# Given tables, a software pipeline and a second copying engine in the S5 input stage of a hybrid encoder

## The chip, the core and the metric

One Trainium2 chip, one of its cores, one program. The metric is the device time of one execution in microseconds (us), the median of several. TensorE (PE) multiplies and transposes, VectorE (DVE), ScalarE (ACT) and GpSimd (POOL) do elementwise work, SyncE (SP) issues most transfers. SBUF is the on-chip memory of 128 partitions; PSUM, eight banks of 128 x 512 fp32, takes what TensorE writes.

## The reference

Two layers over 1040 rows of 1024 numbers. The first has attention beside a state-space layer (S5) whose inputs `u` are turned into complex states by a matrix per group and direction, and then scanned. Of it, this matters here:

```python
a_bar = jnp.exp(a * dt)
b_bar = ((a_bar - 1.0) / a)[..., None] * lax.complex(b_re[direction].astype(f32), b_im[direction].astype(f32))
bu = jnp.einsum('blgp,gnp->blgn', ug.astype(jnp.complex64), b_bar)
_, states = lax.associative_scan(_linear_combine, (a_seq, bu), axis=1, reverse=reverse)
```

There are 64 groups of 16 inputs, 64 states a group, two directions.

## The kernel before

The kernel is a row of stages, each a block with one instruction list per engine and a barrier at its end. Three matter here.

`front` projects the rows: 36 units of 128 output columns, TensorE without a pause. A unit's three pieces sit in PSUM until they are taken out; unit u + 2 writes the same place. Eight units give `u`, four the keys and values, and then come eight heads of three units: `q` (VectorE normalises it, the rows of L1709 to L1718), gate `a` and gate `b` (ScalarE's sigmoid, then VectorE multiplies, L1726). Behind the gates VectorE builds half tables with `complex_table` (six operations of 128 x 512 each, L770 to L775): 16 that a later stage needs (`tab_d`), and `2 * EARLY` for `s5_states` (`tab_in_d`), spread over the gates by `made_after`, two buffers, stored by SP.

`s5_states` makes the inputs of the scan, eight steps of the sequence at a time. The 64 groups go in eight blocks of eight. For a block, a table of powers of `a_bar` times `B` (real and imaginary, 128 x 2 x 8 x 8 x 16) is needed in `table[:, n % 2]`: the first two come from `tab_in_d`, VectorE builds six in a loop of two, 128 x 1024 per operation. TensorE transposes it (L846) in four lots m = 0 to 3 of four transposes into two alternating banks `tp`; ScalarE copies a bank to the weights `wl` ("w_in" in the rows, L874). When all four are copied, TensorE multiplies for each of the eight groups (L855, L857: two column halves for two directions; four matmuls, each of them two records) into one of four banks `zp`, and ScalarE copies that to `Z` (L879). Each engine takes the block's steps in that order, transposes first, then sums, with signals `turned`, `copied`, `summed`, `stored` between them and `built` for tables. `us` holds all of `u`.

`heads` then runs the attention, with the scan of `Z` on GpSimd beside it. `Steps` signals each VectorE operation; called as `do(...)` it makes the next instruction wait for this one, as `do.free(...)` it does not.

Of the kernel before, what the change touches and what calls it, by code (L numbers as in the profile page):

```python
# [21 lines left out]
P = 128  # L22
KC = D // P
HEADS, KV, HD = 8, 2, 128
G, GP, NS = 64, 16, 64
T = P // GP
CH = L // T
# [320 lines left out]
EARLY = 2  # L348
# [429 lines left out]
def s5_states(nc, c, d, t, gates_stored):  # L778

    with stage(nc) as s:  # L780
        us = s.sb("us", [P, G, CH])
        table = s.sb("tab", [P, 2, 2, GB, T, GP])
        tmp = s.sb("tmp", [P, 2, GB, T, GP])
        wl = s.sb("w_in", [P, GB, 2, P])
        tp = [s.ps(f"tp{b}", 512) for b in range(2)]
# [3 lines left out]
        built = s.flag("table_built")  # L789
        turned = s.flag("turned", per=4, credit=8)  # L790
        copied = s.flag("weights_copied", per=4, credit=4)
        summed = s.flag("summed", per=GB, credit=GB)
        stored = s.flag("stored", per=GB, credit=GB)
        steps = s.sem("dve_steps")
        uv = d["u"].rearrange("s p g c -> (s p) g c")
        with nc.Block() as block:  # L796
            @block.sync
            def _(sp):
                for n in range(G // GB):
                    if n < EARLY:  # L800
                        if n:
                            for half in range(2):
# [3 lines left out]
                        for half in range(2):  # L806
                            g = slice(half * GB // 2, (half + 1) * GB // 2)
                            sp.dma_start(table[:, n % 2, :, g].rearrange("p q g s f -> p q (g s f)"),
                                         d["tab_in"][n][:, :, half, :]).then_inc(tab_loaded[half], 16)
                    if n >= 2:  # L810
                        sp.wait_ge(loaded[n % 2], 16 * (n // 2))
                    g = slice(n * GB, (n + 1) * GB)
                    sp.dma_start(us[:, g, :], uv[:, g, :]).then_inc(loaded[n % 2], 16)

            @block.vector
            def _(dve):
                do = Steps(dve, steps)
                do.free(nc.vector.memset(t["Z"][:, 0, :, :], 0.0))
                with do.loop((G // GB - EARLY) // 2, 12) as i:
                    for b in range(2):  # L820
                        n = i * 2 + b + EARLY

                        turned.wait(dve, n, -4)
                        g = bass.ds(n * GB, GB)
                        do(complex_table(nc.vector, do, table[:, b], tmp,
                                         t["pw_in"][:, :, :, g].rearrange("p s q g -> p q s g"),
                                         t["B"][:, :, g, :], 1))
                        dve.sem_inc(built.sem, 1)

            @block.tensor  # L830
            def _(pe):
                turned.start(pe)
                summed.start(pe)
                f, r = slice(0, NS), slice(NS, P)
                for nb in range(G // GB):
                    b = nb % 2
                    if nb >= EARLY:
                        built.wait(pe, nb - EARLY, 1)
                    for m in range(4):
                        if nb < EARLY and m % 2 == 0:  # L840
                            pe.wait_ge(tab_loaded[m // 2], 16 * (nb + 1))

                        copied.wait(pe, nb, m - 1)
                        for n in range(4):
                            g, q = 2 * m + n // 2, n % 2
                            last = nc.tensor.transpose(tp[m % 2][:, n * P:(n + 1) * P],  # L846
                                                       table[:, b, q, g].rearrange("p s q -> p (s q)"), c["ident"][:, :])
                        last.then_inc(turned.sem, 1)
                    copied.wait(pe, nb, 4)
                    pe.wait_ge(loaded[b], 16 * (nb // 2 + 1))  # L850
                    for g in range(GB):
                        stored.wait(pe, nb, g - 3)
                        for q in range(2):
                            cols = slice(q * CH, (q + 1) * CH)
                            nc.tensor.matmul(zp[g % 4][f, cols], wl[:, g, q, f], us[:, nb * GB + g, :],  # L855
                                             start=True, stop=True)
                            last = nc.tensor.matmul(zp[g % 4][r, cols], wl[:, g, q, r], us[:, nb * GB + g, ::-1],  # L857
                                                    start=True, stop=True)
                        last.then_inc(summed.sem, 1)

            @block.scalar
            def _(act):
                copied.start(act)
                stored.start(act)
                for b in range(2):
                    act.wait_ge(gates_stored[b], 16 * HEADS)
                with act.Fori(0, G // GB // 2) as i:
                    for b in range(2):
                        nb = i * 2 + b
                        for m in range(4):  # L870
                            turned.wait(act, nb, m + 1)

                            summed.wait(act, nb, 2 * m + 2 - GB)
                            nc.scalar.activation(wl[:, 2 * m:2 * m + 2, :, :].rearrange("p g q m -> p (g q m)"),  # L874
# [2414 lines left out]
```

## Time and profile before

| | us |
|---|---|
| median of 3 runs (2682.29 to 2682.92) | 2682.81 |
| profiled execution, its own time | 2685.11 |
| its span | 2683.3 |
| PE busy | 2501.9 (93%) |
| DVE busy | 1432.0 (53%) |
| ACT busy | 976.6 (36%) |
| POOL busy | 1145.5 (43%) |

Times in a row count from the start of the span. Busy shares average over all stages; what a change in one stage is worth is read in that stage, from who waits for whom. In a timeline row "x8" is eight instructions merged, the second number the time from the first's start to the last's end, and the bracket the engine's idle time ahead and the work whose end released it.

### The profile page before, as it was taken

Reading aid. Unit: us, or ns where it says so; the run is one execution under the profiler, and the core shown is the slowest. Engines: PE = TensorE matmul, PEld = TensorE weight load, DVE = VectorE, ACT = ScalarE, POOL = GpSimd, SP = SyncE. Lnnn points to the kernel's source line nnn. Section 1 sums busy time; section 2 is a strip of 40 time slices with the busy share of each in tenths; the row PEclk is TensorE's granted clock in tenths of the full one; section 3 lists DMA queues with packets and bytes.
Section 4 is the critical chain, followed back from the end, with each engine's and each line's share of the span. In section 5 each row is a group of like instructions: output and inputs, shape, how many; then the busy total and the mean of one; then the engine's idle time right before and its main releaser. Section 6 shows DMA issues by size and latency. Waiting matters only on the chain. (4 is left out here: it accounts for less than half of the span.)

```text
span 2683.3 us, 40555 instructions
## 1 busy us (share of the span) xinstructions
PE 2501.9 (93%) x15206; PEld 2164.7 (81%) x15206; DVE 1432.0 (53%) x2120; ACT 976.6 (36%) x2130; POOL 1145.5 (43%) x1114
## 2 busy tenths in 40 slices
PE   6999999779998879999999999999898899999998
PEld 6988888678887669777788887887776699999787
DVE  6459887657776545415654543556555452222414
ACT  5232222756664121323332333265565420000331
POOL 3545452067776246322135444343343255554330
PEclk9999999889999989999999999999998899999999
DMA  7424443311112674535333433534334264443544
GB/s 167 106 80 132 145 147 103 117 42 36 49 41 98 160 190 138 192 118 175 98 117 123 151 124 134 177 116 151 136 107 170 73 241 156 143 140 132 171 157 157
DMA packets 272216, 349.27 MB, mean 130 GB/s; under 512 B 45700, under 2 KB 212254, under 8 KB 269990
## 3 DMA queue, kind: packets, MB, share of 16 engines
q1 hardware_dynamic: 236422, 268.85, 32.3%
q10 hardware_dynamic: 35616, 78.00, 8.0%
q8 instruction: 118, 1.93, 0.3%
q14 instruction: 60, 0.49, 0.1%
HBM read 223.23 MB, written 114.03 MB: 126 GB/s over the span
## 5 line engine op out<-in xcount | busy, mean ns | idle before, releaser
L1164 POOL TENSOR_TENSOR w_hi<-w_raw,ones 128x512 fp32r<-128x512 f32 (+1 forms) x232 | 289.0, 1246 | 736.9 <-PE r L1175 324.8
L1175 PE MATMUL r<-h_lo,w_hi 128*128 128x264 f32 (+1 forms) x1200 | 395.6, 330 | 5.1 <-PEq L224 5.1
L1175 PE MATMUL r<-h_hi,w_lo 128*128 128x264 f32 (+1 forms) x1200 | 387.2, 323 | 0.0
L1175 PE MATMUL r<-h_hi,w_hi 128*128 128x264 f32 (+1 forms) x1200 | 386.5, 322 | 0.0
L1166 POOL TENSOR_TENSOR w_lo<-w_raw,w_hi 128x512 fp32r<-128x512 f32 (+1 forms) x232 | 355.2, 1531 | 18.2
L1175 PEld LDWEIGHTS r<-h_lo,w_hi 128*128 128x128 f32 x1200 | 227.2, 189 | 26.6 <-issue 7.6
L1175 PEld LDWEIGHTS r<-h_hi,w_hi 128*128 128x128 f32 x1200 | 227.2, 189 | 21.3 <-issue 2.4
L1175 PEld LDWEIGHTS r<-h_hi,w_lo 128*128 128x128 f32 x1200 | 227.2, 189 | 17.6
L499 POOL TENSOR_TENSOR w_lo<-room,w_hi 128x512 fp32r<-128x512 f32 x64 | 87.1, 1388 | 193.3 <-ACT w_hi L586 193.3
L1905 PE MATMUL o<-v,prob 116*116 116x129 f32 (+1 forms) x1296 | 166.1, 274 | 0.3 <-ACT prob L1955 0.3
L1905 PEld LDWEIGHTS o<-v,prob 116*116 116x116 f32 (+1 forms) x1296 | 158.3, 180 | 3.9 <-ACT prob L1955 0.5
L895 POOL TENSOR_TENSOR scan<-Z,room 128x256 f32<-128x256 f32 x130 | 96.4, 742 | 144.6 <-POOLq L796 100.5
L1175 PE MATMUL sums<-h_lo,w_hi 128*128 128x264 f32 (+1 forms) x432 | 155.5, 360 | 1.7 <-PEq L409 1.7
L1175 PE MATMUL z<-h_lo,w_hi 128*128 128x264 f32 (+1 forms) x384 | 146.7, 382 | 4.9 <-PEq L2220 3.6
L3218 DVE TENSOR_TENSOR buffer<-buffer 128x1040 f32<-128x1040 f32 x16 | 25.4, 1588 | 216.9 <-ACT buffer L3195 216.9
L1175 PE MATMUL sums<-h_hi,w_lo 128*128 128x264 f32 (+1 forms) x432 | 139.7, 323 | 0.0
L1175 PE MATMUL sums<-h_hi,w_hi 128*128 128x264 f32 (+1 forms) x432 | 139.3, 323 | 0.0
L1175 PE MATMUL z<-h_hi,w_hi 128*128 128x264 f32 (+1 forms) x384 | 127.5, 332 | 0.0
L1175 PE MATMUL z<-h_hi,w_lo 128*128 128x264 f32 (+1 forms) x384 | 127.4, 332 | 0.0
L1175 PE MATMUL r<-xc_hi,w_lo 128*128 128x264 f32 (+1 forms) x384 | 123.6, 322 | 0.0
L1175 PE MATMUL r<-xc_hi,w_hi 128*128 128x264 f32 (+1 forms) x384 | 123.1, 321 | 0.0
L1175 PE MATMUL r<-xc_lo,w_hi 128*128 128x264 f32 (+1 forms) x384 | 123.0, 320 | 0.0
(398 smaller groups left out, 6213.9 us busy)
## 6 DMA issues: line engine op xcount, KB each, us to landing
w_raw<-in_w_in_even SPq DMA_DIRECT2D x72, 256.0 KB, 3.4
w_raw<-in_w_in_odd SPq DMA_DIRECT2D x64, 256.0 KB, 3.6
w_raw<-in_w_ogate SPq DMA_DIRECT2D x64, 256.0 KB, 2.7
v_d<-vs ACTq DMA_DIRECT2D x8, 1152.0 KB, 4.2
us<-u_d SPq DMA_DIRECT2D x16, 520.0 KB, 5.4
xc_d<-xc ACTq DMA_DIRECT2D x8, 1040.0 KB, 6.3
qk_d<-qk ACTq DMA_DIRECT2D x16, 520.0 KB, 2.7
qk<-qk_d SPq DMA_DIRECT2D x8, 1040.0 KB, 5.0
```

Source lines behind the costliest of these rows:

```text
L499: nc.gpsimd.tensor_tensor(w[1][:, at % HK, cols], wr[:, at % 2, cols], w[0][:, at % HK, cols].bitcast(F32), ALU.subtract).then_inc(wl_done, 1)
L895: do(tt(tmp[:, :, :, :], now.broadcast_to([P, 2, 2, G]), t["step"][:, :, :].rearrange("p (o q) g -> p o q g", o=2), ALU.mult))
L1164: self.nc.gpsimd.tensor_tensor(hi, raw, one, ALU.mult).then_inc(self.hi_done, 1)
L1166: self.nc.gpsimd.tensor_tensor(lo, raw, hi.bitcast(F32), ALU.subtract).then_inc(self.split, 1)
L1175: ins = self.nc.tensor.matmul(bank[:, 0:n], w[:, u % self.buffers, k, :], z[:, off:off + n], start=(first and k == 0 and w is self.hi and ...
L1905: last = nc.tensor.matmul(o_slot(w)[0:m, :], sb[0:kn, n % NB, k, i * m:(i + 1) * m], vt[0:kn, k, g, :], start=(k == 0), stop=(k == NT - 1))
L3218: do(v.tensor_tensor(og[:, b, :], og[:, b, :], cz[:, b, :], ALU.mult))
```

## The change

`EARLY` goes from 2 to 3: `front` builds six half tables for `s5_states` instead of four, and VectorE builds five tables in the stage instead of six. `table` gets four buffers, `wl` two, `tp` four banks, one for each m; `us` is halved. TensorE's lots of transposes for block nb + 1 are put behind groups 1, 3, 5 and 7 of block nb. VectorE takes the weight copies of m = 3 and, in odd blocks, of m = 2 (`act_copies` says which are ScalarE's), and its table operations are single steps between these copies, five a block. No loops are left.

```diff
-EARLY = 2
+EARLY = 3
...
-        us = s.sb("us", [P, G, CH])
-        table = s.sb("tab", [P, 2, 2, GB, T, GP])
+    NB, HB, TB = G // GB, GB // 2, 4
+
+    def act_copies(nb, m):
+        return m < 2 or (m == 2 and nb % 2 == 0)
+        us = s.sb("us", [P, G // 2, CH])
+        table = s.sb("tab", [P, TB, 2, GB, T, GP])
-        wl = s.sb("w_in", [P, GB, 2, P])
-        tp = [s.ps(f"tp{b}", 512) for b in range(2)]
+        wl = s.sb("w_in", [P, 2, GB, 2, P])
+        tp = [s.ps(f"tp{m}", 512) for m in range(4)]
...
+        def copy_weights(eng, copy, nb, m):
+            eng.wait_ge(turned, 4 * nb + m + 1)
+            if nb >= 2:
+                eng.wait_ge(summed, GB * (nb - 2) + 2 * m + 2)
+            copy(wl[:, nb % 2, 2 * m:2 * m + 2, :, :].rearrange("p g q m -> p (g q m)"),
+                 tp[m][:, :]).then_inc(copied[m], 1)
...
+                        for half in range(2):
+                            if n:
                                 sp.wait_ge(tab_loaded[half], 16 * n)
-                        if n >= 2:
-                            sp.wait_ge(turned.sem, turned.per * (n - 1) + turned.credit)
...
+                    if n >= NB // 2:
+                        sp.wait_ge(summed, GB * (n - NB // 2 + 1))
...
+                def table_step(n, i):
+                    g = slice(n * GB, (n + 1) * GB)
+                    q, second = divmod(i, 3)
+                    if i == 0 and n >= TB:
+                        dve.wait_ge(turned, 4 * (n - TB + 1))
+                    if second == 2:
+                        do(tt(table[:, n % TB, q], tmp[:, 0], tmp[:, 1], ALU.add if q else ALU.subtract))
+                        if q:
+                            dve.sem_inc(built, 1)
+                        return
+                    power = t["pw_in"][:, :, second, g].rearrange("p s g -> p g s").unsqueeze(3)
+                    x = t["B"][:, second ^ q, g, :].unsqueeze(2)
+                    do(tt(tmp[:, second], power.broadcast_to([P, GB, T, GP]), x.broadcast_to([P, GB, T, GP]), ALU.mult))
+
                 do.free(nc.vector.memset(t["Z"][:, 0, :, :], 0.0))
-                with do.loop((G // GB - EARLY) // 2, 12) as i:
-                    for b in range(2):
-                        n = i * 2 + b + EARLY
-
-                        turned.wait(dve, n, -4)
-                        g = bass.ds(n * GB, GB)
-                        do(complex_table(nc.vector, do, table[:, b], tmp,
...
+                for b in range(2):
+                    dve.wait_ge(gates_stored[b], 16 * HEADS)
+
+                def some_steps(first, count):
+                    for at in range(first, min(first + count, 6 * (NB - EARLY))):
+                        table_step(EARLY + at // 6, at % 6)
+
+                for nb in range(NB):
+                    for m in range(4):
+                        if nb:
+                            some_steps(5 * nb + m, 1)
+                        if not act_copies(nb, m):
+                            copy_weights(dve, nc.vector.tensor_copy, nb, m)
+                    if nb:
+                        some_steps(5 * nb + 4, 1)
+                    else:
+                        some_steps(0, 5)
...
+                def turn(nb, m):
+                    if nb < EARLY:
+                        pe.wait_ge(tab_loaded[m // 2], 16 * (nb + 1))
+                    else:
+                        pe.wait_ge(built, nb - EARLY + 1)
+                    if nb:
+                        pe.wait_ge(copied[m], nb)
...
+                for m in range(4):
+                    turn(0, m)
+                for nb in range(NB):
+                    pe.wait_ge(loaded[nb % 2], 16 * (nb // 2 + 1))
                     for g in range(GB):
-                        stored.wait(pe, nb, g - 3)
+                        n = GB * nb + g
+                        pe.wait_ge(copied[g // 2], nb + 1)
+                        if n >= 4:
+                            pe.wait_ge(stored, n - 3)
...
+                        last.then_inc(summed, 1)
+                        if g % 2 and nb + 1 < NB:
+                            turn(nb + 1, g // 2)
...
+                for m in range(4):
+                    if act_copies(0, m):
+                        copy_weights(act, copy, 0, m)
+                for n in range(G):
+                    nb, g = divmod(n, GB)
+                    act.wait_ge(summed, n + 1)
+                    nc.scalar.activation(t["Z"][:, 1:CH + 1, :, n:n + 1].rearrange("p c q g -> p q (c g)"),
+                                         zp[n % 4][:, 0:2 * CH].rearrange("p (q c) -> p q c", q=2),
+                                         ACT.Copy).then_inc(stored, 1)
+                    if g % 2 and nb + 1 < NB and act_copies(nb + 1, g // 2):
+                        copy_weights(act, copy, nb + 1, g // 2)
```

What VectorE has to do in `s5_states` before: one table, in the loop (L770 to L775 are the steps of `complex_table`; ISA and REGISTER_ALU rows are waits and addresses).

```order
L770 ISA [waits turned_129]
L770 REGISTER_ALU
L770 TENSOR_TENSOR tmp<-room 128x1024
L771 ISA
L771 TENSOR_TENSOR tmp<-room 128x1024
L84 ISA
L772 TENSOR_TENSOR tab<-tmp 128x1024 [waits dve_steps_133]
L84 REGISTER_ALU
L773 TENSOR_TENSOR tmp<-room 128x1024 [waits dve_steps_133]
L774 TENSOR_TENSOR tmp<-room 128x1024
L84 REGISTER_ALU
L775 TENSOR_TENSOR tab<-tmp 128x1024 [waits dve_steps_133]
```

And in the changed kernel, in block 1 and the first steps of block 2 (there L841 is a product, L835 a sum or difference, L804 the weight copy; `tp_120` is the bank of m = 2, `tp_121` that of m = 3).

```order
L841 TENSOR_TENSOR tmp<-room 128x1024 [waits dve_steps_138,turned_131]
L841 TENSOR_TENSOR tmp<-room 128x1024 [waits dve_steps_138]
L804 COPY w_in<-tp_120 128x512 [waits turned_131,dve_steps_138]
L835 TENSOR_TENSOR tab<-tmp 128x1024
L804 COPY w_in<-tp_121 128x512 [waits turned_131,dve_steps_138]
L841 TENSOR_TENSOR tmp<-room 128x1024
L841 TENSOR_TENSOR tmp<-room 128x1024 [waits dve_steps_138]
L835 TENSOR_TENSOR tab<-tmp 128x1024 [waits dve_steps_138]
```

Two weight copies have come between the steps; every step waits for the one before it, at the latest through the copy's wait, and no step waits for a copy.

TensorE between two blocks before, from the last group of block 0 (L857) to the first of block 1 (L855), without the repeats of the first lots:

```order
L857 MATMUL zp_123<-us,w_in 64x130
L846 MATMUL tp_118<-ident,tab 128x128 [waits weights_copied_130,table_half0_loaded_126]
L846 MATMUL tp_118<-ident,tab 128x128 x3
L846 MATMUL tp_119<-ident,tab 128x128 [waits weights_copied_130]
L846 MATMUL tp_119<-ident,tab 128x128 x3
L846 MATMUL tp_118<-ident,tab 128x128 [waits weights_copied_130,table_half1_loaded_127]
L846 MATMUL tp_118<-ident,tab 128x128 x3
L846 MATMUL tp_119<-ident,tab 128x128 [waits weights_copied_130]
L846 MATMUL tp_119<-ident,tab 128x128 x3
L855 MATMUL zp_120<-us,w_in 64x130 [waits stored_132,u_loaded1_125,weights_copied_130]
```

The changed kernel, TensorE in block 1 from the end of group 1 to the start of group 4 (L875 is the transpose for block 2, L890 and L892 the matmuls):

```order
L892 MATMUL zp_123<-us,w_in 64x130
L875 MATMUL tp_118<-ident,tab 128x128 [waits weights_copied0_132,table_half0_loaded_128]
L875 MATMUL tp_118<-ident,tab 128x128 x3
L890 MATMUL zp_124<-us,w_in 64x130 [waits stored_137,weights_copied1_133]
...
L892 MATMUL zp_125<-us,w_in 64x130
L875 MATMUL tp_119<-ident,tab 128x128 [waits weights_copied1_133,table_half0_loaded_128]
L875 MATMUL tp_119<-ident,tab 128x128 x3
L890 MATMUL zp_122<-us,w_in 64x130 [waits stored_137,weights_copied2_134]
```

The sixteen transposes that stood together, each lot behind a copy, now stand four at a time behind two groups, and a group waits for its own copy alone.

## Rows read from the trace of the kernel before

**Rows 1.** The page's first line.

```profile
span 2683.3 us, 40555 instructions
```

**Rows 2.** Stretches: length, busy (x) of PE, PEld, DVE, ACT, POOL, clock, DMA.

```profile
272.00:308.00 36.00, 36.00 (x224) 32.13 (x223) 29.92 (x27) 9.68 (x17) 17.88 (x12) 1.00 0.47 140
481.00:487.00 6.00, 5.73 (x60) 5.73 (x62) 5.90 (x6) 3.72 (x7) 0.00 (x0) 0.57 0.81 302
508.00:515.00 7.00, 5.86 (x82) 5.14 (x80) 6.13 (x6) 5.80 (x13) 0.00 (x0) 1.00 0.01 2
```

**Rows 3.** Timeline, ScalarE and GpSimd: start us, us, engine, line, work.

```profile
503.85 1.08 ACT L874 ACTIVATE w_in<-tp 128x512 f32<-128x512 f32 x2 [0.34 <-PE tp L846]
534.14 3.76 ACT L879 ACTIVATE Z<-zp 128x260 f32 x8 [0.85 <-PE zp L857]
...
538.77 0.72 POOL L895 TENSOR_TENSOR scan<-Z,room 128x256 f32<-128x256 f32 x1 [100.49 <-POOLq L796]
```

**Rows 4.** Timeline of TensorE in `s5_states`.

```profile
476.58 0.69 PE L846 MATMUL tp<-ident,tab 128*128 128x128 f32 x2 [8.38 <-DMA tab<-tab_in_d]
...
501.56 1.09 PE L846 MATMUL tp<-ident,tab 128*128 128x128 f32 x8
503.08 1.14 PE L846 MATMUL tp<-ident,tab 128*128 128x128 f32 x8 [0.43 <-ACT w_in L874]
504.99 0.33 PE L855 MATMUL zp<-us,w_in 128*64 128x130 f32 x1 [0.77 <-ACT w_in L874]
...
508.49 0.27 PE L857 MATMUL zp<-us,w_in 128*64 128x130 f32 x1
508.69 0.33 PE L846 MATMUL tp<-ident,tab 128*128 128x128 f32 x1
...
533.34 0.33 PE L855 MATMUL zp<-us,w_in 128*64 128x130 f32 x1 [0.77 <-ACT w_in L874]
...
536.84 0.27 PE L857 MATMUL zp<-us,w_in 128*64 128x130 f32 x1
```

**Rows 5.** Timeline of VectorE in `s5_states`, its first table.

```profile
480.78 1.23 DVE L770 TENSOR_TENSOR tmp<-room 128x1024 f32 x1 [9.11 <-PE tp L846]
481.92 1.22 DVE L771 TENSOR_TENSOR tmp<-room 128x1024 f32 x1
483.18 1.23 DVE L772 TENSOR_TENSOR tab<-tmp 128x1024 f32<-128x1024 f32 x1
...
486.83 1.23 DVE L775 TENSOR_TENSOR tab<-tmp 128x1024 f32<-128x1024 f32 x1
```

**Rows 6.** Timeline of VectorE, two copies from PSUM in the second layer.

```profile
1404.19 0.68 DVE L2460 COPY kt<-sums 128x512 f32<-128x512 f32 x1
1404.79 0.68 DVE L2460 COPY kt<-v 128x512 f32<-128x512 f32 x1
```

**Rows 7.** Timeline of VectorE in `front`, heads 0 to 2.

```profile
195.16 1.96 DVE L1709 TENSOR_TENSOR work<-work,scratch 128x1040 f32<-128x1040 f32 x1
...
215.81 0.69 DVE L770 TENSOR_TENSOR staged<-room,C 128x512 f32<-128x512 f32 x1 [0.15 <-DVE staged L775]
...
223.67 1.84 DVE L1726 TENSOR_TENSOR work<-work,r 128x264 f32<-128x264 f32 x3 [0.15 <-DVE table L775]
...
232.58 2.04 DVE L1709 TENSOR_TENSOR work<-work,scratch 128x1040 f32<-128x1040 f32 x1 [0.22 <-DVE staged L775]
...
267.69 1.77 DVE L1709 TENSOR_TENSOR work<-work,scratch 128x1040 f32<-128x1040 f32 x1 [0.22 <-DVE table L775]
```

**Rows 8.** Timeline of SyncE's issues, tables in `s5_states`.

```profile
471.41 1.26 SPq L808 DMA_DIRECT2D tab<-tab_in_d  x2
...
478.44 1.17 SPq L808 DMA_DIRECT2D tab<-tab_in_d  x2
```

**Rows 9.** Timeline of ScalarE in `front`, last pieces of `q`, heads 1 and 2.

```profile
227.53 0.48 ACT L1467 ACTIVATE work<-r,cols_a 128x264 f32<-128x264 f32 x1 [1.74 <-PE r L1175]
...
263.55 0.48 ACT L1467 ACTIVATE work<-r,cols_a 128x264 f32<-128x264 f32 x1 [1.74 <-PE r L1175]
```

More of the change, by code:

```diff
@@ L788, in s5_states @@
         tab_loaded = [s.sem(f"table_half{half}_loaded") for half in range(2)]
[L789 to L793, printed above, removed]
+        built = s.sem("table_built")
+        turned = s.sem("turned")
+        copied = [s.sem(f"weights_copied{m}") for m in range(4)]
+        summed, stored = s.sem("summed"), s.sem("stored")
         steps = s.sem("dve_steps")
         uv = d["u"].rearrange("s p g c -> (s p) g c")
+        def copy_weights(eng, copy, nb, m):
[4 more added lines that the diff above has]
+                 tp[m][:, :]).then_inc(copied[m], 1)
         with nc.Block() as block:
@@ L817, in _ @@
                 do = Steps(dve, steps)
[L818 to L828 removed]
+                tt = nc.vector.tensor_tensor
@@ L830, in _ @@
             @block.tensor
             def _(pe):
-                turned.start(pe)
-                summed.start(pe)
                 f, r = slice(0, NS), slice(NS, P)
[L835 to L850, printed above, removed]
+                def turn(nb, m):
[5 more added lines that the diff above has]
+                        pe.wait_ge(copied[m], nb)
+                    for n in range(4):
+                        g, q = 2 * m + n // 2, n % 2
+                        last = nc.tensor.transpose(tp[m][:, n * P:(n + 1) * P],
+                                                   table[:, nb % TB, q, g].rearrange("p s q -> p (s q)"), c["ident"][:, :])
+                    last.then_inc(turned, 1)
@@ L858, in _, with copy @@
                                                     start=True, stop=True)
-                        last.then_inc(summed.sem, 1)
+                        last.then_inc(summed, 1)
+                        if g % 2 and nb + 1 < NB:
+                            turn(nb + 1, g // 2)
             @block.scalar
             def _(act):
-                copied.start(act)
-                stored.start(act)
+                def copy(out, given):
+                    return nc.scalar.activation(out, given, ACT.Copy)
@@ L865, in _ @@
                 for b in range(2):
                     act.wait_ge(gates_stored[b], 16 * HEADS)
[L867 to L874, printed above, removed]
-                                                 tp[m % 2][:, :], ACT.Copy).then_inc(copied.sem, 1)
-                        for g in range(GB):
-                            summed.wait(act, nb, g + 1)
-                            gg = bass.ds(nb * GB + g, 1)
-                            nc.scalar.activation(
-                                t["Z"][:, 1:CH + 1, :, gg].rearrange("p c q g -> p q (c g)"),
-                                zp[g % 4][:, 0:2 * CH].rearrange("p (q c) -> p q c", q=2),
-                                ACT.Copy).then_inc(stored.sem, 1)
+                for m in range(4):
+                    if act_copies(0, m):
+                        copy_weights(act, copy, 0, m)
```

16 lines of the change are left out of this document (6 added, 10 removed).

## The prediction

> **What bounds the kernel now.** The profiled execution has a span of 2683.3 us [rows 1]; its own time was 2685.11 us, 1.8 above the span, and 2.3 above the median of the three timed runs, 2682.81. The change is worth what it takes out of, or adds to, that span.
>
> I read the busy time by stretches first, to see who is the bound where the edits fall. In the projection stage ahead (`front`) TensorE is busy 36.00 of 36.00 us at full clock while VectorE has 29.92; in `s5_states` nobody is full: 5.86 of 7.00 us for TensorE, 6.13 for VectorE, 5.80 for ScalarE at a clock of 1.00 [rows 2]. So `front` is TensorE's and the reader should ask there only whether VectorE's extra work can make TensorE wait. `s5_states` is a chain of waits, and its end is what counts: the first scan on GpSimd starts at 538.77, 0.87 after ScalarE's last copy of Z ends, and everything behind starts from that barrier [rows 3]. A microsecond off the stage is a microsecond off the kernel.
>
> Then TensorE's own timeline, where the loop repeats. Block 4's transposes start at 508.69, block 3's at 501.56: 7.13 us a block [rows 4]. Inside: eight transposes in 1.09 (the last lasts 0.27, so one per 0.117), 0.43 idle for a copy of the weights, eight more, 0.77 idle for the last copy, then 3.70 of matmuls (504.99 to 508.69). Without the idle stretches TensorE needs 3.70 + 16 x 0.117 = 5.57. The eight blocks end at 536.84 + 0.27 = 537.11, the last one's matmuls having begun at 533.34, so 3.77 [rows 4]; ScalarE's last copy ends 0.79 later, at 537.90 [rows 3].
>
> VectorE in the same stage has no copies. It waits until the first block is turned and builds from 480.78 [rows 5]. TensorE's waits inside a block are all put down to ScalarE's copies [rows 4], so VectorE, busy 6.13 of 7.00, is near the bound and not the bound.
>
> **What the change does to each engine.** TensorE does the same 128 transposes and 256 matmuls. What goes is its idle time for the copies: four transposes of the next block stand behind every second group, into a bank of their own, and the weights have two buffers. That removes 0.43 + 0.77 = 1.20 a block. It adds switches between transposes and matmuls, eight a block for two. A switch costs about 0.09: from the last matmul at 508.49 to the transpose at 508.69 is 0.20, where the 32 matmul pairs of a block follow in 3.70 / 32 = 0.116 [rows 4]. Bounds: nothing, and 0.2; I take 0.09, so 6 x 0.09 = 0.5, and 6.1 us for a block nobody holds up.
>
> VectorE loses one table of six but takes twelve of the 32 weight copies (bank 3 of every block, bank 2 of every odd one; of these 9 lie before its last table step). A table step now always waits for the step before: start to start 1.26 (481.92 to 483.18), against 1.14 where the old code let the second product follow the first freely (480.78 to 481.92) [rows 5]. 30 steps x 1.26 = 37.8. The trace has no VectorE copy from `tp`, but it has the same shape from another PSUM tile: 0.68 each, the next starting after 0.60 [rows 6]. A step behind a copy does not wait for it (the order rows show no wait there), so 0.60 stands for a copy; the bounds are 0.60 and 0.72 (0.69 plus a waited gap of 0.03). Signalling a finished table costs 0.12 more: the gap in front of a step behind a signal is 0.15 where others have 0.03 [rows 7].
>
> *Does VectorE keep up?* From block 1 to block 5 it does 5 steps and 1 or 2 copies: 5 x 1.26 + 0.60 = 6.9 or 7.5, mean 7.2 with the signals 7.3. TensorE needs 6.1. So VectorE becomes the bound there, at the old pace of 7.13, and the removed waits come back as TensorE waiting for copies 2 and 3 of each block. The gain can come only from the end, when VectorE has no steps left.
>
> *The sum.* VectorE's first instruction is the copy of bank 3 of block 0, which waits for the same four turned banks as its first product now, 480.78. Nothing ahead of that event changes but a half table asked for earlier. Step 0 starts at 481.38. Copy (5, 3) has 29 steps, 7 further copies and 4 signals in front of it: 481.38 + 36.54 + 4.20 + 0.48 = 522.60. It ends at 523.29 and TensorE goes on 0.06 later, at 523.35 (as at 504.99 behind ScalarE's copies, which ended at 503.85 + 1.08 = 504.93 [rows 3, 4]). Then two groups (0.93), four transposes (0.47), two switches (0.18): 524.93. Block 6 is free, 6.1: 531.03. Block 7 has no transposes behind it, 3.77: 534.80. Now it is 537.11. **Gain 2.3 us**, 2682.81 - 2.3 = 2680.5.
>
> ScalarE in the free blocks has 8 copies of Z and 2 or 3 of weights. Its eight Z copies take 3.76, the last lasting about 0.67, so at most 0.44 each; weight copies in a pair (1.08 for two) follow after 0.48 [rows 3]. 8 x 0.44 + 3 x 0.48 = 5.0, under 6.1: no bound.
>
> *Loads.* Table 0 is asked for from 471.41, and TensorE's wait for its first half ends at 476.58; table 1 is asked for at 478.44, when the second half is there [rows 4, 8]. So a half table lands 5 to 7 us after its issue. The change asks for table 1's first half at 476.6, for table 2 at about 482 to 484, and has it by about 491. TensorE would turn it from about 489.5, but stands at copy (1, 2) until VectorE ends it: 481.38 + 8 x 1.26 + 0.12 + 0.69 = 492.3. A load some microseconds late costs nothing, since VectorE's copies wait only for transposes due some 5 us before them. The halved `us` makes loads 4 to 7 wait for sums four blocks earlier; each has over 20 us.
>
> *The front.* Two more half tables are built, two more stores. One took 7.9 (215.81 to 223.67) [rows 7]; half of a table of this stage would be 3.6 (below), so 4 to 8 each. A head with three builds and its normalisation took VectorE 35.1 (232.58 to 267.69), and TensorE takes 36.02 for one (227.53 to 263.55) [rows 7, 9]. The change gives heads 2 and 5, which had two, a third; so every head but the last takes VectorE some 35.1, and it still gains 0.9 a head on TensorE. What TensorE needs is the first piece of the second gate: in head 0 it came at 223.67 for a need at 227.53. In head 1, two builds now stand in front of that piece instead of one: 232.58 + (223.67 - 195.16) = 261.1 for a need at 263.5. Slack 2.4, so the price is nothing.
>
> *A rule weighed.* [rows 5] show 1.14 for a product that waits for nothing and 1.26 for one that waits. The Trainium skill (VectorE: DVE Perf Modes, The DRAIN you can't avoid) says that instructions drain all the same and a semaphore between them costs nothing. By that rule a step would cost the mean of now, (488.06 - 480.78) / 6 = 1.21; 30 of them 36.4, and the result 2679.1. I keep the rows' 1.26, since all 30 now wait.
>
> **Rivals.**
>
> *TensorE free all through (0.06).* If steps cost less than I think, TensorE runs at its own pace: block 0, half of it at the low clock (between 5.6 and twice that), 8.5 from 480.6; six blocks of 6.1; then 3.77: 529.5. Gain 7.6, 2675.2. It needs 30 steps and 8 copies in some 38 us, 1.1 a step; no step in [rows 5] is under 1.14.
>
> *The stage breaks even or loses (0.10).* VectorE's chain has no slack at all, so every cost I have too low counts 8 to 30 times. Copy and step share no buffer, but a copy at 0.90 start to start instead of 0.60, for whatever reason, gives 8 x 0.3 = 2.4 and no gain; at 1.1, the time is 2684.5. For it: no row has a PSUM copy followed by a product. Against: the pair in [rows 6], PSUM then PSUM, at 0.60.
>
> *The front is exposed (0.04).* Once VectorE is more than the 2.4 of slack later in a head than I put it, TensorE waits for the gate's eviction and every further microsecond counts. With both added builds exposed at 4: 2680.5 + 8 = 2688.5, slower. Against: heads with three builds catch up, 35.1 to 36.0.
>
> *The clock falls (0.02).* TensorE's clock was 0.57 in 481 to 487, after 8.38 us idle up to 476.58, and 1.00 in 508 to 515 with 17% idle [rows 2, 4]; 1.00 is the 2.4 GHz level, 0.57 mostly the 1.2 GHz one. With idle stretches of 0.5 to 1.4 a block it should stay. If it sat at 1.2 GHz, a block would be nearly twice 5.6, about 11, for five blocks: 20 us more, 2700. The Trainium skill (TensorE: Matmul & The Clock Gate, Part 4: PE-mode transpose) says that transposes do not count as busy for the gate, which speaks for it, as they now stand between all matmuls. By that rule, the trace should already show less than 1.00 with a third of the work in transposes, and it doesn't.
>
> **How the numbers follow.** My forecast, VectorE the bound in blocks 1 to 5 and the end gained: 0.78, with 2678.9 to 2682.3: down by 1.5 if a step costs today's mean of 1.21 (1.21 x 30 against 37.8), up by 1.0 if a copy costs 0.72, and either way by switches (7 to 9 of them in the free part, each 0.1 off). With break-even taken in on one side and half-way to the first rival on the other, 2677.8 to 2683.2 holds 8 in 10. What a measurement of this kernel can tell is 0.2%, 5.4 us: a gain over that is only the first rival, a loss over that the front or the clock. Faster 0.07, same 0.88, slower 0.05.
>
> **What would show it.** VectorE without a gap over 0.2 from 480.8 to about 524; its copies at 0.68 to 0.69 and 0.60 to the next start; TensorE idle about 0.8 to 1.4 a block until then, released by VectorE's copies and not ScalarE's, and no more in blocks 6 and 7, 6.1 from one to the next; the last matmul near 534.8; `front` at the same 36.0 a head. It would be wrong if steps behind copies start late, if ScalarE's copies hold TensorE, or if the stage begins at another time than 471.4.

## The result: 0.16% slower, and the profile after

The median of 20 runs is 2687.6 us (2683.06 to 2690.45); the kernel before, on the same chip and in the same rounds, has 2682.57 (20 runs). The ratio of after to before is 1.0016, with a 95% interval of 1.0010 to 1.0022: 4.3 us lost (2.7 to 5.9), where a gain of 2.3 was forecast. The profiled executions hide it: 2684.87 us after, 2685.11 before, one from the faster end of its runs and one from the slower. So the total of two traces says nothing here; their stages do.

The page after, span and first lines of the busy times:

```profile
span 2683.0 us, 40407 instructions
PE 2498.3 (93%) x15206; PEld 2155.9 (80%) x15206; DVE 1459.9 (54%) x2138; ACT 972.8 (36%) x2118; POOL 1137.9 (42%) x1114
```

Three stretches to set beside those of [rows 2] (a head of the front, the stage's first block with the clock coming back, its middle; each row is the length, then the busy time of PE, PEld, DVE, ACT and POOL, the clock, and the DMA share and rate):

```profile
276.00:312.00 36.00, 36.00 (x224) 32.13 (x223) 33.64 (x32) 9.55 (x18) 17.97 (x12) 1.00 0.43 141
485.00:491.00 6.00, 5.02 (x62) 3.93 (x58) 5.86 (x6) 4.23 (x8) 0.00 (x0) 0.96 0.76 259
508.00:515.00 7.00, 5.96 (x74) 4.63 (x74) 6.68 (x7) 5.57 (x11) 0.00 (x0) 1.00 0.17 65
```

VectorE has 33.6 of 36.0 us in a head where it had 29.9 (this head has a third build now), and 6.68 of 7.00 in the stage where it had 6.13.

**Two landmarks** cut the program. The front is taken from TensorE's first turn of `c` (116.65 us before, 118.62 after; that start differed by 1.0 and 1.4 us between the two traces of each of these kernels, and lies at 116.5 to 119.0 in all) to VectorE's memset of Z. The stage of the states is taken from that memset to GpSimd's first scan (538.77 in [rows 3]). After:

```profile
475.87 0.17 DVE L843 MEMSET Z<- 128x128 f32 x1 [3.10 <-PEq L1320]
541.02 0.72 POOL L928 TENSOR_TENSOR scan<-Z,room 128x256 f32<-128x256 f32 x1 [99.45 <-POOLq L807]
```

and before, the memset that the 538.77 stands against:

```profile
471.51 0.17 DVE L818 MEMSET Z<- 128x128 f32 x1 [2.42 <-PEq L1287]
```

So the front went from 471.51 - 116.65 = 354.9 to 475.87 - 118.62 = 357.2 us, **2.4 longer**, and the stage from 67.3 to 65.1, **2.1 shorter**.

**The stage runs as forecast.** VectorE in it, and the end of its work there:

```profile
484.89 0.69 DVE L804 COPY w_in<-tp 128x512 f32<-128x512 f32 x1 [8.85 <-PE tp L875]
485.50 2.48 DVE L841 TENSOR_TENSOR tmp<-room 128x1024 f32<-128x1024 f32 x2
488.01 1.23 DVE L835 TENSOR_TENSOR tab<-tmp 128x1024 f32<-128x1024 f32 x1
...
495.68 0.69 DVE L804 COPY w_in<-tp 128x512 f32<-128x512 f32 x1
496.29 1.22 DVE L835 TENSOR_TENSOR tab<-tmp 128x1024 f32<-128x1024 f32 x1
...
526.79 0.69 DVE L804 COPY w_in<-tp 128x512 f32<-128x512 f32 x1
```

A copy lasts 0.69 and the next instruction starts 0.61 after it starts; two steps take 2.51 (485.50 to 488.01). Copy (5, 3) starts 41.90 behind the first copy; the forecast's sum has 522.60 - 480.78 = 41.82. Besides the loads of the two first tables (9.2 and 1.0 us), what TensorE waits for is VectorE, 3.5 us in all:

```profile
PE tp L875 <- DMA tab<-tab_in_d: 10.2, 2, 9.2
PE zp L890 <- DVE w_in L804: 3.5, 8, 0.9
```

and its end (the first row goes on behind copy (5, 3); the last one is the last matmul):

```profile
527.53 0.33 PE L890 MATMUL zp<-us,w_in 128*64 128x130 f32 x1 [0.16 <-DVE w_in L804]
...
528.57 0.66 PE L875 MATMUL tp<-ident,tab 128*128 128x128 f32 x4
529.16 0.33 PE L890 MATMUL zp<-us,w_in 128*64 128x130 f32 x1
...
530.20 0.66 PE L875 MATMUL tp<-ident,tab 128*128 128x128 f32 x4
...
539.15 0.27 PE L892 MATMUL zp<-us,w_in 128*64 128x130 f32 x1
```

A pair of groups with its four transposes takes 1.63 (528.57 to 530.20) where nobody holds it, so a free block takes 6.5 and not 6.1.

**The front does not.** VectorE, heads 1 and 2 of 0 to 7 (start, us; the idle time in brackets). The row of line 1742 opens a head's normalisation, as those of line 1709 do in [rows 7]; 263.13 is the first piece of head 1's second gate:

```profile
234.55 2.04 DVE L1742 TENSOR_TENSOR work<-work,scratch 128x1040 f32<-128x1040 f32 x1 [0.22 <-DVE staged L775]
...
263.13 1.84 DVE L1759 TENSOR_TENSOR work<-work,r 128x264 f32<-128x264 f32 x3
...
273.04 1.24 DVE L1742 TENSOR_TENSOR work<-work,scratch 128x1040 f32<-128x1040 f32 x1 [0.22 <-DVE table L775]
...
288.69 0.69 DVE L770 TENSOR_TENSOR staged<-room,C 128x512 f32<-128x512 f32 x1
...
292.08 1.77 DVE L774 TENSOR_TENSOR staged<-room,C 128x512 f32<-128x512 f32 x1
...
300.53 1.26 DVE L1759 TENSOR_TENSOR work<-work,r 128x264 f32<-128x264 f32 x2
...
310.02 1.24 DVE L1742 TENSOR_TENSOR work<-work,scratch 128x1040 f32<-128x1040 f32 x1 [0.22 <-DVE staged L775]
```

Head 1 takes VectorE 38.49 us (234.55 to 273.04) and head 2 takes 36.98, where TensorE needs 36.02: it is idle for 0.52 at most in a row in head 2, and falls behind. An operation of 128x512 values lasts 0.69 alone (288.69) and up to 1.77 while GpSimd splits weights beside it (292.08):

```profile
291.69 1.61 POOL L1199 TENSOR_TENSOR w_lo<-w_raw,w_hi 128x512 fp32r<-128x512 f32 x1
```

The Trainium skill (GPSIMD Engine Reference, 2. Architecture) says that GpSimd's read port to SBUF is shared with VectorE; the 0.69 and 1.77 agree. Over the 132 such operations of the 22 builds in this trace, all 77 that overlap no work of GpSimd last 0.68 to 0.69 us, and the 55 that do have a mean of 1.45, a few of them at 0.69 too. No run took the splits away, so the cause of the 1.77 is read from this overlap.

Who is held by a late gate piece of VectorE is ScalarE, ahead of its roots (waits in the front, then its timeline):

```profile
ACT L1525 <- DVEq L1760: 5.9, 5, 1.4
```

```profile
301.54 0.48 ACT L1500 ACTIVATE work<-r,cols_a 128x264 f32<-128x264 f32 x1 [1.74 <-PE r L1208]
...
303.26 1.28 ACT L1525 ACT_TABLE_LOAD   x1 [0.95 <-DVEq L1760]
...
337.56 0.48 ACT L1500 ACTIVATE work<-r,cols_a 128x264 f32<-128x264 f32 x1 [1.74 <-PE r L1208]
...
373.96 0.48 ACT L1500 ACTIVATE work<-r,cols_a 128x264 f32<-128x264 f32 x1 [1.74 <-PE r L1208]
...
410.31 0.48 ACT L1500 ACTIVATE work<-r,cols_a 128x264 f32<-128x264 f32 x1 [1.74 <-PE r L1208]
```

The rows of line 1500 follow TensorE's last piece of `q` in a head, as [rows 9] do. They are of heads 3 to 6. Up to 337.56 they are 36.02 apart, then 36.40 and 36.35, and 36.69 to head 7: behind head 4, VectorE's lateness has reached TensorE. These are 1.4 of the 2.4 us; the rest comes behind that. In the heads of the trace before, no wait of ScalarE is for VectorE's gate.

### The profile page after: what moved, and what is told of

It is laid out like the page before. It is cut to its first block and busy times, and to the rows that moved or that the text cites. A ratio compares the mean times of both kernels' runs of the same rounds, so it can differ in the third digit from the quotient of the medians.

```text
span 2683.0 us, 40407 instructions
## 1 busy us (share of the span) xinstructions
PE 2498.3 (93%) x15206; PEld 2155.9 (80%) x15206; DVE 1459.9 (54%) x2138; ACT 972.8 (36%) x2118; POOL 1137.9 (42%) x1114
```

## The experiments

"Front" and "stage" are the lengths between the landmarks in each run's own trace; the ratio is to the kernel before in the same rounds. Lines with + and - are against the changed kernel unless another base is named.

| kernel | front | stage | median, us (runs) | ratio, 95% interval |
|---|---|---|---|---|
| before, unchanged (`base_again`) | 354.9 | 67.1 | 2683.63 (11) | 0.9999, 0.9989 to 1.0008 |
| `after_again` | 357.2 | 65.1 | 2688.88 (11) | 1.0018, 1.0009 to 1.0027 |
| `front_only` | 357.3 | 64.9 | 2687.11 (11) | 1.0007, 0.9998 to 1.0016 |
| `early_start` | 354.9 | 62.7 | 2682.08 (11) | 0.9995, 0.9986 to 1.0004 |
| `front_four` | 359.4 | 64.0 | 2687.97 (9) | 1.0022, 1.0012 to 1.0032 |
| `one_then_two` | 354.9 | 65.4 | 2682.80 (11) | 1.0004, 0.9995 to 1.0013 |
| `three_ahead` | 357.2 | 62.4 | 2683.41 (11) | 1.0005, 0.9996 to 1.0014 |
| `late_stage` | 355.7 | 67.3 | 2685.22 (11) | 1.0012, 1.0003 to 1.0021 |
| `warm_before` | 354.9 | 64.8 | 2680.67 (11) | 0.9998, 0.9989 to 1.0007 |
| `warm_after` | 357.3 | 65.5 | 2687.27 (9) | 1.0021, 1.0011 to 1.0031 |
| `both_mended` | 354.9 | 62.4 | 2684.06 (11) | 0.9999, 0.9990 to 1.0008 |
| `both_warm` | 354.9 | 62.4 | 2683.45 (11) | 1.0002, 0.9993 to 1.0011 |
| `warm_before_2` | 354.9 | 67.4 | 2682.53 (12) | 0.9995, 0.9985 to 1.0005 |
| `warm_one` | 354.9 | 63.9 | 2683.84 (12) | 1.0004, 0.9995 to 1.0012 |
| `stage_alone` | 354.9 | 77.1 | 2693.80 (6) | 1.0038, 1.0023 to 1.0052 |
| `fewer_steps` | 354.8 | 59.7 | 2677.29 (12) | 0.9978, 0.9970 to 0.9987 |

**Both kernels again**, to see what repeats.

> The kernel before once more, unchanged, with a trace of its own. It tells how far one traced execution of the same program differs from another, stage by stage. Theory A (the front pays for the tables): the last sigmoid of the projection stage near 468, the first scan near 539, as in the first trace, within 0.5 us; what differs by more is no property of the change. Rival B (the traces of before and after differ by chance in the front too): the front end moves by 2 to 4 us here as well.

> The changed kernel once more, with a second trace. A: again about 4 us slower than before in the median; TensorE's heads 3 to 7 of the front again over 36.0 us each, 1.7 us in sum, and the stage with the tables again 1.8 us shorter. B: the front's lateness is elsewhere or absent in this trace.

The loss repeats (1.0018), and so do front and stage to 0.2 us. What does not repeat is behind the stage: from the first scan to the end the two traces of before differ by 3 us (2144.5 and 2141.6), and the two of after as well (2142.0 and 2145.1). That stretch is 2141.4 to 2145.4 in the seven traces with the old stage code and 2140.1 to 2149.2 in the eleven with the new. So a total of one trace can't show a difference of a few us, and the medians of the runs have to.

**The front alone.** The kernel before, with a third given table built and stored, not used:

```
+GIVEN = 3
-    jobs = [("out", n) for n in range(2 * G // GB)] + [("in", n) for n in range(2 * EARLY)]
+    jobs = [("out", n) for n in range(2 * G // GB)] + [("in", n) for n in range(2 * GIVEN)]
```

> Only the front builds and stores the third table's two halves (GIVEN = 3), spread over the gates as in the change; the stage behind is that of before and reads two tables, so the third is stored and not used. A: the front pays, so this is slower than before by the change's loss plus the 1.8 us that the stage gained, 4 to 6 us (2687 to 2689). Rival C (the stage or what it leaves behind pays, not the front): within 1 us of before. The prediction on record said 0 for this part.

The 2.4 us of the front are all there. The run shows less than was expected: by its ratio 1.9 us (-0.5 to 4.3) over the kernel before, where 4 to 6 had been expected, and by itself that excludes neither theory. The stage, whose code is the old one, took 64.9 instead of 67.1 to 67.3, which nobody expected; it is taken up below. Front and stage together take 422.2 us here and 422.1 in the kernel before: in this trace the stage gave back what the front lost.

**A fourth table in the front** (`GIVEN = 4` on the same base).

> The stage stays as before and loads two tables; the front builds and stores four of them (24 half tables instead of 20), two of which nobody reads. Theory A (VectorE's work is what bounds heads 1 to 6 of the front once it has three builds in each): heads 0 and 5 get a fourth build of some 5.5 to 6 us that has no slack left to lie in, so the front from the first turn of c to the Z memset takes some 357.3 + 6 to 11 = 363 to 368 us against 354.9 of the kernel before and 357.3 with three tables, and the run some 2692 to 2697 us. Rival B (a cost of 2.4 us that comes once, from one late gate or one late load of ScalarE's table): the front takes 357 to 358 us and the run stays near 2687.

The front grew by 2.1 more, not by 6 to 11. So VectorE's total is not simply the bound (theory A as stated falls), and neither does the cost come once only (rival B falls).

**The same 22 half tables, one behind gate a and two behind gate b**, where the change has two and one:

```
-        made_after[gates[n * (len(gates) - 1) // NX]].append(n)
+        made_after[gates[n // 3 * 2 + (n % 3 > 0)]].append(n)
```

> The changed kernel, with the 22 half tables put one after a head's gate a and two after its gate b in heads 0 to 6 (the last after the last gate a, as it was). The work is the same, only its place among the heads' steps is another. Theory A (the sum of VectorE's work in a head, 36 to 38.5 us, against TensorE's 36.02): the front still takes 356.5 to 358 us, and the run 2686 to 2689. Rival C (what costs is two builds in a row between gate a and the next step that ScalarE waits for): the front falls back to 354.9 to 355.5 us, and the run to some 2684 to 2686.

The front is at 354.9 again and the run at 1.0004: rival C holds, and decides the front. VectorE's busy time from 200 to 454 us, some seven heads, first in this kernel, then in the changed one:

```profile
sum 254.00, DVE 227.07; mean DVE 32.44
```

```profile
sum 254.00, DVE 239.31; mean DVE 34.19
```

That is 12.2 us more. From the first step of head 0 to that of head 7, where the list of operations is the same, it is 240.9 against 223.5 us. Of these 17.4 us, 11.5 are in the builds: as many of their operations lie beside work of GpSimd (52 here, 55 in the changed kernel), but with a mean of 1.27 us and not 1.45. So the edit shows that the place alone costs the 2.4 us; that it does so through GpSimd's splits is read from the overlaps. Three pairs differ by this edit, with other things the same: `after_again` (1.0018) and this one (1.0004), `three_ahead` and `both_mended` (1.0005, 0.9999), `warm_after` and `warm_one` (1.0021, 1.0004). The mean is 0.0012, 3.3 us, against 2.4 in the traces.

**VectorE started earlier.** `early_start` has two given tables; VectorE does 7 steps before its first copy and ScalarE takes bank 2 of every block. `three_ahead` has three tables and 6 steps ahead; `both_mended` is that with the other placement in the front.

```
-EARLY = 3
+EARLY = 2
-        return m < 2 or (m == 2 and nb % 2 == 0)
+        return m < 3
+                some_steps(0, 7)
...
-                            some_steps(5 * nb + m, 1)
+                            some_steps(2 + 5 * nb + m, 1)
```

> The stage of the change with two given tables as before, so the front is that of before. VectorE begins its first seven steps at once, without waiting for the copy of bank 3 of block 0, and takes only the copies of m = 3; ScalarE takes three banks of every block. A: the front costs nothing here and VectorE has 9 us of lead, so TensorE runs at its own 6.5 us a block; the stage ends about 5 us earlier than before and the kernel takes 2677 to 2679. C: if the pipelined stage costs something behind it, it stays within 2 us of before.

> The changed kernel, with three given tables, but VectorE does the six steps of its first table ahead of its first copy, where it stood idle for 9 us, and stays four steps further ahead from there. If the stage's rest is still VectorE's steps between TensorE's blocks, the time from the Z memset to the first scan falls from 65.1 us to 62.5 to 64, and the run to some 2683 to 2686; the front stays at 357.3 us. If the stage is bound by TensorE and ScalarE now, it stays at 65 us and the run does not change. Beside two given tables with an early start (62.8 us in the stage, 354.8 in the front) it tells what the third table costs by itself: about 2.4 us by theory A.

> The changed kernel with both mends: the half tables one behind gate a and two behind gate b, and VectorE's first six table steps ahead of its first copy. If the two are independent the front takes 354.9 us, the stage 62.4 to 62.7, and the run ends 4.7 us before that of the kernel before by its traces (67.2 in the stage), 2.5 where its clock is back early: ratio 0.998 to 0.999, some 2678 to 2680.5 us. If the later parts take back what the stage gives, as the sums of traces and medians did not agree so far by 1 to 3 us, it is at 2681 to 2683.

VectorE's 9 idle us at the stage's head are worth 2.7 us in the stage between `after_again` and `three_ahead`, and 3.0 between `one_then_two` and `both_mended`. With two given tables the early start makes 62.7 us of the 77.1 that `stage_alone` takes (below). But `early_start` missed its time: its run is 1.3 us below the kernel before (-3.8 to 1.1), where 4 to 6 had been expected; "within 2 us of before" is what its rival had said. The two mends add up in the trace (354.9 and 62.4), but not in the run: 0.9999, where 0.998 to 0.999 was expected. In that trace everything behind the first scan took 2149.2 us, 5 to 8 more than in the two of before, and no run tells why.

**A pure delay.** The kernel before, with two more multiplications behind its last gate:

```
+                for n in range(2):
+                    do(v.tensor_tensor(rs, rs, rs, ALU.mult))
```

> The kernel before, with two multiplications of 128x1040 values on VectorE added behind its last gate, so that the stage of the states starts some 2.7 us later and nothing else is changed. If a delay only adds up, the median is 2.5 to 3 us above that of the kernel before in the same rounds (ratio 1.0010). If a shift ahead of the stage makes what follows longer too (TensorE's clock falling at other places), it is 4 to 7 us above it (ratio 1.0015 to 1.0026), which would be the part of the changed kernel's loss that front and stage do not explain.

They take 2.52 us, but 1.8 of it hid in VectorE's wait for the stage's start (2.42 us before, 0.60 now), so the front grew by 0.8 only. The interval (0.8 to 5.6 us) holds that, and it holds more: inconclusive on whether a shift costs more than itself.

**TensorE kept busy before its first table**, the result not used. In `warm_before` on the kernel before, in `warm_after`, `both_warm`, `warm_one` on the changed kernel, on `both_mended` and on `one_then_two`:

```
+                for n in range(20):
+                    nc.tensor.transpose(zp[3][:, 0:P], c["ident"][:, :], c["ident"][:, :])
```

The reason is in the clock column (the third value from a row's end). In the kernel before, block 0 is summed at the 1.2 GHz level up to some 486 us:

```profile
480.00:483.00 3.00, 2.23 (x19) 1.83 (x19) 2.22 (x2) 1.41 (x3) 0.00 (x0) 0.50 0.84 268
483.00:487.00 4.00, 4.00 (x48) 4.00 (x46) 3.90 (x5) 3.06 (x6) 0.00 (x0) 0.60 0.81 315
```

and in `front_only`, with the same stage code, it is back at 2.4 GHz before the first product at 485.47:

```profile
484.00:487.00 3.00, 2.23 (x32) 1.83 (x32) 2.01 (x2) 1.88 (x4) 0.00 (x0) 0.87 0.95 316
487.00:491.00 4.00, 3.48 (x52) 3.10 (x47) 3.93 (x4) 4.00 (x9) 0.00 (x0) 1.00 0.89 301
```

In all seven traces with the old stage code the two go together: the clock back 14 to 15 us behind the memset and a stage of 67.1 to 67.4 us in four (`before`, `base_again`, `late_stage`, `warm_before_2`), back 7 to 9 us behind it and 64.0 to 64.9 in three (`front_only`, `front_four`, `warm_before`). VectorE's first table ends at 488.06 and its second begins at 490.21 in the kernel before, 2.2 us later; in `front_only` it is 492.27 and 492.75, 0.5.

> The kernel before, with 20 transposes of the identity added at the head of TensorE's program of the stage, where it otherwise stands idle for 5 us until the first table has landed; their result is not used. In the traces of the kernel before TensorE's clock is at its half level from 1 to 15 us behind the Z memset, and VectorE's second table starts 2.2 us later behind its first than it does where the clock is back 2 to 3 us sooner. Theory (half of what the changed kernel's stage seemed to gain is that state of the clock and not the change): with the clock back before block 0 the stage as it was takes 64 to 65 us from the Z memset to the first scan instead of 67.1 to 67.3, and the run 2680 to 2681 instead of 2682 to 2683. Rival (VectorE's pace alone sets the stage): it stays at 67 and the run does not change.

> The changed kernel with the same 20 idle transposes added. Its stage took 65.1 us with TensorE's clock back at full at the first product and 65.4 with it back 2 us after it, so by the theory it does not depend on the clock in block 0: it stays at 64.8 to 65.2 us, the front at 357.2, and the run at 2687 to 2688.5. Rival (TensorE's first block is on the path in it too): the stage falls by 1 us or more.

> The kernel with both mends and the 20 idle transposes. Its stage has VectorE ahead, so TensorE's first block at the half clock is on the path: with the clock back earlier the stage falls from 62.5 to 60.5 to 61.8 us and the run by some 1 to 1.5 us. If VectorE's steps or ScalarE's copies are the bound in it all the same, it stays at 62.4.

> The kernel before with 20 idle transposes ahead of its first table, once more, as the base for the next one: the stage takes 64.8 us again from the Z memset to the first scan, the front 354.9, and the run is 1.4 to 2.5 us below the kernel before.

> The changed kernel with one half table behind gate a and two behind gate b, and the 20 idle transposes: front 354.9 us, and TensorE's clock the same in block 0 as in the run before this one. Theory (at the same clock the pipeline neither gains nor loses): the stage takes 65.0 to 65.4 us, 0.2 to 0.6 more than the 64.8 of the old stage, and the run is within 1 us of the run before this one or a little above it. Rival (the pipeline gains 2 us by itself): 62.5 to 63.5 us, and 2 us below it.

In `warm_before` the old stage took 64.8 us, as expected; its run, at 0.9998, did not show the 2 us. In `warm_before_2`, the same kernel, the clock was late all the same and the stage took 67.4: the transposes don't fix the clock, but the pair shows that one code takes 64.8 or 67.4 with it. The changed stage took 65.5 in `warm_after`, with the clock back when it was without the transposes, and 63.9 in `warm_one`, which missed its expectation by 1.1. There the clock was back 4 us behind the memset and low once more from 11 to 14, so its block 0 had not the clock of `warm_before_2`, which the comparison had asked for. Where the stages are compared with a clock back early, the old one has 64.0 to 64.9 and the new one, without VectorE's steps ahead, 63.9 to 65.5: the pipeline gains nothing that is clear. In no trace with the new stage code was the clock as late as 14 us, so what the new stage takes then isn't known. `both_warm` stayed at 62.4 with the clock at full from block 0's first product, as its second expectation had it: with VectorE ahead, TensorE's first block is not the limit either. The runs say the same: `warm_one` is 1.3 us above `warm_before_2` by the medians, with intervals that overlap, and `one_then_two` (no front loss, new stage) stands at 1.0004 (0.9995 to 1.0013).

**What bounds the new stage.** `stage_alone` has `EARLY = 2`; `fewer_steps` is `one_then_two` without the four multiplications of tables 4 and 6, so those tables hold wrong values:

```
+                    if n % 2 == 0:
+                        return
```

> The changed stage with two given tables as before, so VectorE builds six tables, 36 steps, between its copies; the front as before at 354.9 us. If VectorE's steps are the bound, six more steps of 1.24 us add 6 to 7.5 us to the 65.1: 71 to 73 us, longer than the old stage's 67.2, and the run is at some 2687 to 2690. If the stage is bound by something else, it stays under 67.

> As the changed kernel with one half table behind gate a and two behind gate b, but VectorE leaves out the four multiplications of tables 4 and 6 (8 of its 30 steps; those two tables hold wrong values). If VectorE is the bound of the stage up to some 3 us, beyond which TensorE and ScalarE are, the stage falls from 65.4 us to 61.5 to 62.5, as with VectorE ahead. If it is VectorE's alone, it falls by 8 x 1.24 = 9.9 us to 55.5.

With two given tables, the new stage takes 77.1 us, 12.0 more for six steps of 1.25, where 6 to 7.5 more had been expected; the run is 10.2 us above the kernel before. TensorE now waits for whole tables:

```profile
PE tp L875 <- DVEq L837: 10.2, 5, 3.0
```

With 8 steps less it takes 59.7, 5.7 less than `one_then_two`, between the two values expected: VectorE is the bound for that much, and in this trace TensorE no longer waits for it. (Its clock was also back 3 us sooner than in `one_then_two`, so the 5.7 may not be VectorE's alone.) The run follows (5.5 us below `one_then_two`'s median, in other rounds). So this pipeline as it stands needs the third given table. The table is not the only way to give VectorE that lead: `early_start` has two and takes 62.7, with its first seven steps in the 9 us in which VectorE was idle and bank 2's copies left to ScalarE.

## Why the prediction was wrong, by its steps

**"Slack 2.4 in head 1, so the price is nothing"** is the step that failed: the cost of a head with three builds was taken as 35.1 us wherever they stand. The time of the one piece that the prediction looked at was right: 261.1 was forecast for head 1, and with the later start of the front (1.97 us) the 263.13 of the trace is that to 0.1. What came behind it was not. Head 1 took VectorE 38.49 us and head 2 36.98 in place of 35.1, so instead of gaining "0.9 a head" on TensorE's 36.02 it lost 2.5 and 1.0, which used up the slack; TensorE is late behind head 4. A build's six operations are 0.69 each beside an idle GpSimd and up to 1.8 beside its splits, so neither the 7.9 of a build nor the 35.1 of a head is fixed. The front cost 2.4 us in every trace with three tables so placed (4.5 with four) and nothing in the traces with one build behind gate a and two behind gate b, or with two tables (`late_stage` apart, which has its own delay). That settles the place; that it is the whole 3.3 us of the runs is not shown.

**"Nothing ahead of that event changes"** failed with it: the stage starts 2.4 us later.

**VectorE's pace** (step 1.26, copy 0.60, signal 0.12) was right: 41.90 against 41.82. So was ScalarE as no bound, and the loads: one wait of 1.0 us for table 1 that the copies hid. TensorE waited 3.5 us for VectorE's copies, some 0.7 a block where 0.8 to 1.4 had been expected. The rule weighed (1.21 a step) is refuted by 2.51 for two.

**A free block of 6.1** was mis-sized; it takes 6.5, so in the forecast's own terms the six added switches cost (6.5 - 5.57) / 6 = 0.16 each and not 0.09. From the memset to the last matmul's end the forecast had 534.80 - 471.51 = 63.3; it came to 63.55.

**The gain of 2.3 in the stage** was right by the two traces (2.1) and wrong as an expectation of the run. It was worked out against a trace in which block 0 of the old stage ran at the low clock. The old code with the clock back early takes 64.0 to 64.9, and the new one 65.1. So the 2.1 us go with the clock. Whether the change itself brings it back sooner is open: both kernels with the old stage behind a longer front (`front_only`, `front_four`) had it early too, and of the five traces with the old stage behind the front at 354.9 to 355.7 four had it late. The rival "the stage breaks even or loses" came nearest for the stage, by another mechanism than the costly copies it named.

**The rival "the front is exposed"** had the right mechanism, with a chance of 0.04. Its bound of 8 us was too high, since 2.4 was exposed; with no gain in the stage, 2.4 alone would have given 2685.2. The clock did not fall in the blocks (1.00 in 508 to 515, with transposes between all matmuls), so that rival falls. What it took from the Trainium skill (TensorE: Matmul & The Clock Gate, Part 4: PE-mode transpose), that transposes do not count as busy, has left no sign in this mix.

**What stays open.** By the traces of before and after, front and stage make 2.4 - 2.1 = 0.3 us. Against an old stage with an early clock (64.9), front 2.4 and stage 0.2 make 2.6 of the 4.3 us (2.7 to 5.9). One more place shows in every trace: TensorE's wait named "issue" ahead of `lag_zero`, first matmul of a later stage. It sums to 5.7 to 6.8 us in the seven traces with the old stage code, and to 6.5 to 9.0 in the eleven with the new one, mean 6.1 and 7.4. Three of them (the kernel before, the changed one, `both_warm`):

```profile
PE lag_zero L1063 <- issue: 6.2, 2, 3.4
```

```profile
PE lag_zero L1096 <- issue: 6.7, 2, 3.6
```

```profile
PE lag_zero L1099 <- issue: 9.0, 2, 5.9
```

The 1.3 us between the means would close the sum to within the interval, but the two ranges overlap and no run took it away, so it is a candidate and not shown. How often the clock is late in block 0 in executions without a trace isn't known either; if in the kernel before it were always late, 2 more us would be missing.

## What to carry to other kernels

Work put "under" a busy engine costs what it takes at the new place, so read the spread of its durations (0.69 to 1.8 us here) and what runs beside it, not one instance; moving one build a head past a gate was worth 2.4 us for nothing. And before a stage's gain is credited, look at TensorE's clock at its start in both traces: here a 2 us gain stood against a late clock in the one before.

## What the hardware showed that was not expected

With the same stage code, TensorE's clock came back before block 0 was summed or only near the end of that, and the idle time ahead of the first table does not tell which: it was 8.4 us in the kernel before, where it came late, 9.1 in `front_only`, where it came early, and 9.15 in `late_stage`, where it came late. Over a whole execution the time at the low level differed by some 20 us between the two profiled kernels (about 150 before, 130 after, summed from the clock column), and the spans were still 2683.3 and 2683.0.

The same list of VectorE's operations over seven heads took 240.9 or 223.5 us, 8% apart, by the place of the builds alone.
